# Chunked delta rule: token transpositions ahead of the first inverse level, and new values as the inverse times (values less decayed keys times state)

## What is computed

```python
    qc, kc, vc = to_chunks(q), to_chunks(k), to_chunks(v)
    decay = jnp.cumsum(gc, axis=-1)
    gamma = jnp.exp(jnp.where(incl, diff, -jnp.inf))
    kb = kc * bc[..., None]
    vb = vc * bc[..., None]
    a_mat = jnp.where(strict, jnp.einsum('bnhid,bnhjd->bnhij', kb, kc) * gamma, 0.0)
    t_mat = triangular_solve(eye + a_mat, eye, left_side=True, lower=True)
    u = jnp.einsum('bnhij,bnhjd->bnhid', t_mat, vb)
    w = jnp.einsum('bnhij,bnhjd->bnhid', t_mat, kb * jnp.exp(decay)[..., None])
    ...
    def step(S, inp):
        qd, kd, u_, w_, qk_, l_ = inp
        v_new = u_ - jnp.einsum('bhcd,bhde->bhce', w_, S)
        o = jnp.einsum('bhcd,bhde->bhce', qd, S) + jnp.einsum('bhij,bhje->bhie', qk_, v_new)
        S = S * l_[..., None, None] + jnp.einsum('bhcd,bhce->bhde', kd, v_new)
        return S, o
```

## Time and profile before

| | us |
|---|---|
| median of 3 runs | 1842.6 (1842.48 to 1845.2) |
| the profiled execution | 1842.54 |
| its span in the trace | 1840.8 |
| PE busy in the span | 1752.9 (95%) |
| DVE busy in the span | 834.1 (45%) |

### The profile page before, as it was taken

The page is one execution under the profiler, slowest core; times in us unless marked ns, Lnnn a source line. Parts: engine busy times, 40 slices in busy tenths (PEclk is TensorE's granted clock), DMA queues, the critical chain, the costliest instruction groups (busy, mean ns, idle before and its releaser), DMA issues.

```text
span 1840.8 us, 26847 instructions
## 1 busy us (share of the span) xinstructions
PE 1752.9 (95%) x10357; PEld 1404.9 (76%) x10357; DVE 834.1 (45%) x1436; ACT 675.7 (37%) x1414; POOL 710.8 (39%) x436
## 2 busy tenths in 40 slices
PE   6999999999997788999999999999999999999999
PEld 5888878877776674567877777888888888888887
DVE  4289878611126787565563354321331332233133
ACT  5366587688841223665045723010001001001000
POOL 4332234433344441563362235434334433442441
PEclk9999999999997999899999999999999999999999
DMA  7230111232212012002201001111111111111112
GB/s 237 59 80 24 35 35 46 58 99 74 91 47 82 2 60 103 1 2 92 69 28 53 24 23 46 46 46 48 54 34 57 46 49 53 46 46 46 57 34 91
DMA packets 112027, 102.33 MB, mean 56 GB/s; under 512 B 5131, under 2 KB 99390, under 8 KB 111678
## 3 DMA queue, kind: packets, MB, share of 16 engines
q1 hardware_dynamic: 109630, 92.67, 16.6%
q10 hardware_dynamic: 2304, 8.39, 1.1%
HBM read 87.42 MB, written 13.63 MB: 55 GB/s over the span
## 4 chain that ended last, share of the span: by engine, by line
PE 88%; DVE 6%; ACT 2%; issue 2%; POOL 1%; DMA 1%; DVEq 0%; ACTq 0%; POOLq 0%
PE ps L1445 9%; PE ps L1447 9%; PE ps L1446 9%; PE ps L437 7%; PE ps L439 7%; PE ps L438 7%; PE ps L409 6%; PE ps L410 6%; PE ps L411 6%; PE ps L987 2%; PE ps L1118 2%; PE ps L1276 2%; PE ps L1301 2%; PE ps L1287 2%; PE ps L939 2%
## 5 line engine op out<-in xcount | busy, mean ns | idle before, releaser
L754 POOL TENSOR_TENSOR WS<-WR,zero 128x1024 fp32r<-128x1024 f32 (+1 forms) x119 | 227.3, 1910 | 878.9 <-PE ps L411 299.0
L756 POOL TENSOR_TENSOR WS<-WR,WS 128x1024 fp32r<-128x1024 f32 (+1 forms) x119 | 302.3, 2541 | 9.3
L1445 PE MATMUL ps<-HS,WS 128*128 128x512 f32 x704 | 274.7, 390 | 3.2 <-DVE HS L345 3.2
L1447 PE MATMUL ps<-HS,WS 128*128 128x512 f32 x704 | 274.3, 390 | 0.0
L1446 PE MATMUL ps<-HS,WS 128*128 128x512 f32 x704 | 274.2, 389 | 0.0
L456 DVE TENSOR_TENSOR X<-X,ps 128x512 f32<-128x512 f32 x272 | 184.6, 687 | 155.9 <-PE ps L439 155.9
L409 PE MATMUL ps<-HS,WS 128*128 128x512 f32 (+2 forms) x560 | 215.4, 385 | 3.9 <-ACT raw L1569 3.9
L410 PE MATMUL ps<-HS,WS 128*128 128x512 f32 (+2 forms) x560 | 212.6, 380 | 0.0
L411 PE MATMUL ps<-HS,WS 128*128 128x512 f32 (+2 forms) x560 | 212.2, 379 | 0.0
L2278 DVE TENSOR_TENSOR prod<-sil,ps 128x512 f32<-128x512 f32 x44 | 30.2, 687 | 394.7 <-PE ps L1447 394.7
L1796 ACT ACTIVATE sil<-ps 128x512 f32<-128x512 f32 x44 | 26.3, 598 | 395.0 <-PE ps L1447 395.0
(11 more groups left out here) (308 smaller groups left out, 2991.6 us busy)
## 6 DMA issues: line engine op xcount, KB each, us to landing
WR<-in_w_gu SPq DMA_DIRECT2D x44, 512.0 KB, 3.8
WR<-in_w_in SPq DMA_DIRECT2D x36, 512.0 KB, 3.7
WR<-in_w_down SPq DMA_DIRECT2D x22, 512.0 KB, 3.6
X<-in_x SPq DMA_DIRECT2D x8, 1024.0 KB, 8.3
dsa_spill<-cacc ACTq DMA_DIRECT2D x12, 512.0 KB, 2.6
KW<-in_w_xkv SPq DMA_DIRECT2D x8, 512.0 KB, 5.0
WR<-in_w_out SPq DMA_DIRECT2D x8, 512.0 KB, 3.7
out<-X SPq DMA_DIRECT2D x8, 512.0 KB, 2.6
```

The lines of the kernel that those rows point to most:

```text
L754: pool.tensor_tensor(hi, w, bc(zero1[:, 0:1], [P, cols]), ALU.add).then_inc(w_hi, 1)
L756: pool.tensor_tensor(lo, w, hi.bitcast(F32), ALU.subtract).then_inc(w_split, 1)
L1445: pe.matmul(ps[:, b0 + half, :], lo, HS[:, 0, k, c], start=(k == 0), stop=False)
L1447: mm = pe.matmul(ps[:, b0 + half, :], hi, HS[:, 0, k, c], start=False, stop=(k == KT - 1))
```

## The change

The parts of batches 1 to 3 come in another order: `k` and `v` now stand before the levels, in `PREP`; batch 0 keeps its order in `FIRST`. Part `w`, `nkbd` and `wTt` are gone. In their place a new step `of_keys` multiplies the keys by the state on PE into a free part of a PSUM bank (four matmuls a chunk), and DVE forms `rhs` from it (two instructions of 128x128: times `ned`, plus `vb`); `new_v` is then a single product of the inverse with `rhs`. In the scan of a chunk `of_keys` and `from_state` come first, then a part, `new_v`, a part, `to_state`, a part, `out`, a part. Because `kD` is loaded over the keys early, ACT copies the keys of chunks 8 to 15 into `kept` once (part `rest` of batch 0). POOL masks level 1 (`X1`) before it makes `Xm`, the first `Am` waits for one slice less (`hs_done` 3 instead of 4), `threshold`'s counts move from parts 10 to 14 of batch 0 to parts 13 to 15, and some entries of `MASKS` move by one part. ACT's `squares` run after `from_state` instead of `new_v`. SP's three loads wait for the same parts, the last for `TT5` in place of `w1`.

```diff
-        PREP = (["gq", "x0"] + [f"{x}{s}" for s in (1, 2, 3) for x in "yz"]
-                + ["k", "y4", "z4", "v", "y5", "z5", "w", "next"])
+        FIRST = (["gq", "x0"] + [f"{x}{s}" for s in (1, 2, 3) for x in "yz"]
+                 + ["k", "y4", "z4", "v", "y5", "z5", "rest", "next"])
+        PREP = ["gq", "k", "x0", "v"] + [f"{x}{s}" for s in LV for x in "yz"] + ["rest", "next"]
+        def tok_bank(b, part, j):
+            return (0 if b and part == "k" else 3) if j else 1
...
             for c in range(SEQ // CHUNK):
-                run(new_v, c)
+                run(of_keys, c)
+                run(from_state, c)
                 if c < 12:
                     b, parts = c // 4 + 1, PREP[4 * (c % 4):4 * (c % 4) + 4]
                     prep(b, parts[0])
+                    run(new_v, c)
+                    prep(b, parts[1])
                     run(to_state, c)
-                    prep(b, parts[1])
-                    run(from_state, c)
                     prep(b, parts[2])
                     run(out, c)
                     prep(b, parts[3])
                 else:
                     tail(2 * (c - 12))
+                    run(new_v, c)
                     run(to_state, c)
-                    run(from_state, c)
                     run(out, c)
                     tail(2 * (c - 12) + 1)
...
             gp.wait(sp, "k1", 3)
+            sp.wait_ge(keys_kept, 1)
             sp.dma_start(kD[:, :, :], back[1]).then_inc(qk_in[1], 16)
...
-            gp.wait(sp, "w1", 3)
+            gd.wait(sp, "TT5", 3)
             sp.dma_start(qD[:, :, :], back[0]).then_inc(qk_in[0], 16)
...
                     gd.wait(pool, "A", b)
+                    level(b, 1)
                     if b == 0:
                         pool.wait_ge(hs_done, 4)
...
-                elif part == "w":
-                    gd.wait(pe, "TT5", b)
-                    for ul in range(8):
-                        for par in range(2):
...
-                            mm = pe.matmul(ps[:, 2 + par, c], nkbd[r, ul * P:(ul + 1) * P], TTm[r, B, c],
...
+            def of_keys(c):
+                if c == 0:
+                    return
+                if c == 8:
+                    pe.wait_ge(keys_kept, 1)
+                sd_.wait(pe, "S", c - 1)
+                for ul, hl, hh, r in pairs_of(c):
+                    w0, h = c % 8 * P + CHUNK * hh, 2 * hh + hl
+                    k = both(4, hl)[:, w0:w0 + CHUNK] if c < 8 else kept[:, hl, w0:w0 + CHUNK]
+                    mm = pe.matmul(ps[r, 6, (2 + hl) * P:(3 + hl) * P], k, S[:, c % 2, h * P:(h + 1) * P],
+                                   start=(hl == 0), stop=(hl == 1), skip_group_check=True)
+                kp_.mark(mm, "ks", c - 1)
...
+                else:
+                    qa_.wait(pe, "qs", c - 1)
+                    rd_.wait(pe, "rhs", c - 1)
+                for ul, hl, hh, r in pairs_of(c):
+                    v = rhs[r, hl * P:(hl + 1) * P] if c else vb[r, B, ul * P:(ul + 1) * P]
+                    mm = pe.matmul(ps[r, 4, hl * P:(hl + 1) * P], TTm[r, B, ul * CHUNK:(ul + 1) * CHUNK], v,
+                                   start=(hl == 0), stop=(hl == 1), skip_group_check=True)
...
+                elif part == "rest" and b == 0:
+                    for hl in range(2):
+                        ins = act.activation(kept[:, hl, :], both(4, hl)[:, SEQ:2 * SEQ], ACT.Copy)
+                    ins.then_inc(keys_kept, 1)
...
-            MASKS = {15: [(2, "count"), (2, "tie")], 16: [(2, 0), (2, 1)], 17: [(2, "kept"), (2, "out")],
+            MASKS = {15: [(2, "count"), (2, "tie")], 16: [(2, 0), (2, 1)], 17: [(2, "kept")], 18: [(2, "out"), (2, "bias")],
...
-                if p == 10:
+                if p == 13:
...
+                    for hl in range(2):
+                        ul = 2 * (c % 4) + hl
+                        ins = dve.scalar_tensor_tensor(rhs[:, hl * P:(hl + 1) * P], ps[:, 6, (2 + hl) * P:(3 + hl) * P],
+                                                       ned[:, 2 * c + hl:2 * c + hl + 1],
+                                                       vb[:, c // 4 % 2, ul * P:(ul + 1) * P], ALU.mult, ALU.add)
```

More of the change, by code:

```diff
@@ L92, in sem, with steps @@
             return ctx.enter_context(nc.semaphore(name))
-        def steps(name, names):
-            return Steps(sem(name), names)
+        def steps(name, names, first=None):
+            return Steps(sem(name), names, first)
         ps = ctx.enter_context(nc.psum_tensor("ps", [P, 8, BANK], F32))
@@ L179, in build_layer @@
         blk = at("blk", [P, 2, 8 * BANK], 56)
-        kdec, vb, wTt = (blk[:, :, 2 * i * BANK:2 * (i + 1) * BANK] for i in range(3))
+        kdec, vb = (blk[:, :, 2 * i * BANK:2 * (i + 1) * BANK] for i in range(2))
         TTm, QKm = blk[:, :, 6 * BANK:7 * BANK], blk[:, :, 7 * BANK:8 * BANK]
-        nkbd = at("nkbd", [P, 8 * P], 96)
+        kept = at("kept", [P, 2, SEQ], 88)
+        rhs = at("rhs", [P, 2 * P], 80)
         Tm = at("Tm", [P, BANK], 100)
@@ L594, in bc_bank, with gdn_order @@
             return e % 3 if e < 8 else e % 2
-        def gdn_order(prep, tail, new_v=None, from_state=None, to_state=None, out=None, beside=None):
+        def gdn_order(prep, tail, new_v=None, from_state=None, to_state=None, out=None, beside=None, of_keys=None):
             def run(step, c):
@@ L603, in gdn_order @@
             prep(-1, "next")
-            for part in PREP:
+            for part in FIRST:
                 run(beside, part)
@@ L1101, in prep @@
                     for j in range(2):
[L1102 to L1108, removed]
+                        bank, src = tok_bank(b, part, j), 4 if part == "k" else 8
+                        if b == 0:
+                            gd.wait(pe, f"kd{j}" if part == "v" else "Q", b)
+                        elif part == "k":
+                            if j:
+                                ga.wait(pe, "gam", b)
+                            else:
+                                gd.wait(pe, "TT5", b - 1)
+                        else:
+                            gd.wait(pe, "Q" if j else "kd0", b)
                         for q in range(4):
@@ L1261, in tail @@
                     o_tr(3 * (h - 5) // 2 + 2)
-            gdn_order(prep, tail, new_v, from_state, to_state, out, beside)
+            gdn_order(prep, tail, new_v, from_state, to_state, out, beside, of_keys)
             for t in range(T_ON, TT):
@@ L1638, in prep @@
                     ga.mark(act.activation(Ym[:, :], ps[:, 0, :], ACT.Copy), part, b)
-                elif part == "w":
-                    if b >= 2:
-                        sp_.wait(act, "o", 4 * (b - 1) - 1)
-                    for j in range(2):
-                        gp.wait(act, f"w{j}", b)
-                        ga.mark(act.activation(wTt[:, B, j * BANK:(j + 1) * BANK], ps[:, 2 + j, :], ACT.Copy),
-                                f"w{j}", b)
+                elif part == "rest" and b == 0:
+                    for hl in range(2):
+                        ins = act.activation(kept[:, hl, :], both(4, hl)[:, SEQ:2 * SEQ], ACT.Copy)
+                    ins.then_inc(keys_kept, 1)
             def squares(t):
@@ L2153, in prep_and_masks @@
                     dve.sem_inc(masks_made, 1)
-            gdn_order(prep_and_masks, tail, to_state=to_state, out=out)
+            gdn_order(prep_and_masks, tail, to_state=to_state, out=out, of_keys=of_keys)
             mean_o(1, T_ON, TT)
```

82 lines of the change are left out of this document (37 added, 45 removed).

## The result

| | kernel before | changed kernel |
|---|---|---|
| median, us | 1842.6 (4 runs, 1842.5 to 1845.2) | 1861.2 (4 runs, 1860.9 to 1862.4) |
| profiled execution, span, us | 1840.8 | 1859.1 |
| mean granted clock (1.00 is PE's full speed) | 0.976 | 0.963 |

The ratio is 1.0099, with a 95% interval of 1.0081 to 1.0116. The forecast was 9.3 us faster; it is 18.6 us slower (1.0%), outside the range and of the other sign.

What follows compares the result with a forecast made beforehand. PE, busy 95% of the span, was taken as the bound, so gains come from its work or waits. Terms summed to 11.3 us, less 2 for the clock: 9.3 gained, 1833.2 us, range 1827.5 to 1840.

Steps and rivals of the forecast that it cites:

- 1 first level: First level of batch 0: `Am` no longer waits for slice 3 and `y1` starts earlier; 2.7 us gained.
- 2 `z4` to `Am` 1: From `z4` of batch 0 to `Am` of batch 1: 18.98 us before, 14.1 after; 4.9 us gained.
- 3 batch 1: Batch 1, `Am` to `Am`: longer way to `z1`, shorter levels; 43.7 us before, 40.3 after, 3.4 gained.
- 4 batch 2: Batch 2: later `z1`, but no `w` product; 37.3 us before, 34.6 after, 2.7 gained.
- 5 batch 3 to chunk 12: Batch 3 to `to_state` of chunk 12: late `rhs` and square root; 37.4 us before, 38.9 after, 1.6 lost.
- 6 tail: Tail: `to_state` waits for ACT's `vn` in chunks 13 to 15, one `from_state` moved ahead; 0.8 us lost.
- reserve of 0 to 4 us for the clock: Batches 2 and 3: products slower after the new waits; 2 us taken off the gain, between 0 and 4.
- wrong sign: At chunk 12, a stall of more than 3 us would show the forecast wrong.
- The price of `rhs`: DVE's two `rhs` steps a chunk: between 0.5 and 1.7 us, taken as 0.55.
- The rule that speaks against it: Mask steps beside POOL's products ahead of `y1` run longer: two meetings a batch at 0.8 us, 4.8 us, giving 1838.0.
- The one that ended slower: One more passage per chunk, `rhs` late by 1.2 us in all 15 chunks: 18 us lost, 1849; chance 0.09.
- Rival c: POOL and DVE meet and PE is cold after each stall: 1838.0 us; chance 0.18.

Runs made afterwards that it cites:

- filled pause: Changed kernel with five added float32 matmuls on PE around `new_v` of chunk 12, three before and two behind, output unread; 1839.5 us, ratio 0.9993.
- late square root: Changed kernel with tile 7's last three mask steps moved into the tail and ACT's square root moved from tail piece 0 to 1; 1834.9 us.
- first level alone: Kernel before, with only POOL making `X1` before `Xm` and `Am` waiting for one slice fewer; 1843.4 us, ratio 1.0013.

## Why the prediction was wrong, step by step

Against the profiled executions (us gained; the last product of the projection stood 0.7 us earlier after than before, which no step claims):

| step | predicted | measured | from |
|---|---|---|---|
| 1 first level | +2.7 | +2.6 | `z4` at 557.83 against 561.17, less 0.7 |
| 2 `z4` to `Am` 1 | +4.9 | +4.8 | 14.18 against 18.98 |
| 3 batch 1 | +3.4 | -0.9 | 44.58 against 43.73 |
| 4 batch 2 | +2.7 | +1.2 | 36.13 against 37.28 |
| 5 batch 3 to chunk 12 | -1.6 | -3.3 | 40.68 against 37.38 |
| 6 tail | -0.8 | -24.1 | 61.0 against 36.9 |
| projection, and behind the logits | 0 | +1.4 | 0.7 each |

**The step that failed** is the sixth, the tail, with the reserve of 0 to 4 us for the clock that was to cover it. I priced the clock by its cost behind one wait inside a batch (about 1.5 us), and in the tail I counted the waits on `vn` (0.48 us each, as measured) but not the clock at which its products run. Step 5 even forecast the late `rhs` and the square root ahead of `vn`. What a fall of the clock there costs stood nowhere in the sum: 32 us of PE work become 55. The filled pause measures it, 21.7 us with every path left as it was; with the clock up the tail took 37.8 us, so the 0.8 of the step (36.9 to 37.7) was right for that clock. That a gain at the end of chunk 15 passes through whole did hold, to 0.7 us. The fair comparison with the forecast of 1833.2 us is the kernel with the filled pause, 1839.5 us: 6.3 us above it, and only just inside the range. That the late square root gave 1834.9, 1.7 from the forecast, is luck, since it also took 3.5 us off the way to chunk 12, by clearing two waits that step 5 had counted as lost.

I had also named the wrong sign for it: a stall at chunk 12 of more than 3 us. The waits were 0.78 and 1.23 us, with PE busy 0.66 us in 2.3, and the clock fell in the second of them; the third, 0.47 us, came behind the fall. Small waits one behind the other were enough, while the kernel before passed the same seam with PE busy 3.3 to 3.8 us in each 4.

**Steps 1 and 2** were right to 0.1 us: `y1` at 539.10 (forecast 539.8, less 0.7 for the projection), the projection's matmuls at 0.39 to 0.40 us behind it, `Am` of batch 1 at 572.01 (572.5). Even so, the run with the first level alone shows that 2.7 us won there need not arrive: the same edit delays `Tm` in the later batches by 2.1 us in all, which step 1 left out, and dips of the clock took some 2.6 us more.

**Step 3** was right up to `z1` (`y1` 9.8 us after `Am`, forecast 9.3; `z1` 15.3, forecast 15.1), and 4.1 us short from `z1` to `Am` of batch 2: 29.3 us, not 25.2. I had walked the levels at the full clock. `z1` itself and `y2` ran at 1.95 and 1.80 us instead of 1.15, and there were waits of 1.23 us on POOL's mask at `y3` and of 1.20 us on `rhs` at chunk 2, behind which `z3` ran at 1.98. **Steps 4 and 5** missed by 1.5 and 1.7 us, step 5 behind the wait of 4.61 us at chunk 9. The price of `rhs` (0.55 us a pair) was right: pairs took 0.56 to 0.61.

**The rule that speaks against it.** A mask step beside POOL's products was again slower. DVE, a step of 512 columns beside POOL and one of 640 with POOL idle:

```profile
593.64 1.42 DVE L1937 SCALAR_TENSOR_TENSOR score<-tieW,negdist 128x512 f32<-128x512 f32 x1
...
609.33 0.82 DVE L1937 SCALAR_TENSOR_TENSOR score<-tieW,negdist 128x640 f32<-128x640 f32 x1
```

POOL at the same time (`Sl`, then a level mask), and its next level mask, beside `rhs` and small steps of DVE:

```profile
593.03 1.48 POOL L865 TENSOR_TENSOR Sl<-S,lastb 128x512 f32<-128x512 f32 x1 [7.89 <-DVE S L2096]
594.47 1.71 POOL L826 TENSOR_TENSOR gam<-Am,Lev 128x512 f32<-128x512 f32 x1
597.49 1.27 POOL L826 TENSOR_TENSOR gam<-Am,Lev 128x512 f32<-128x512 f32 x1 [1.30 <-PE ps L1135]
```

Both are longer, DVE by some 0.7 us (1.42 less 512/640 of 0.82) and POOL's mask by 0.4. The Trainium skill ("SBUF — State Buffer", section "SBUF: two separate sides") describes the shared port as an exclusive lock; these rows agree. But the kernel before has such steps too, and no run isolates the meetings, so how much of steps 3 to 5 is theirs stays open.

**The rivals.** The one that ended slower had the wrong mechanism: `rhs` late in all 15 chunks. It was late by over 2 us in chunks 1, 5 and 9, and elsewhere by at most 1.25 us. Its 1849 was also too low. Rival c had the clock, but only within the batches, and its 1838.0 comes near the 1839.5 of the filled pause. The missing rival was that of the seam: a pause before the tail, 24 us, decided by about 2 us of idle time. Its rows were in the trace of before: L1207 at 1.07 us with the clock at 1.00, and inside the batches single waits after which products ran at 1.97.

## What to carry to other kernels

Before moving a wait, look at what PE does behind it. Here a fall of the clock inside a batch cost one or two microseconds, but ahead of the long tail of small products it cost the whole stretch at half speed. (The products of the batches are small too, and the clock came back in them; what about the tail's keeps it down was not isolated, only that eight dense ones raised it.) Price each seam by that, as a case of its own and not as a reserve, and keep the work of other engines off whatever releases PE there. A change that makes room in a dependency chain may pay only when the side work is placed anew, as here, so judge it after that.

## What the runs showed of the hardware that was not expected

- The granted clock stayed at 0.50 for 61.0 us while PE was busy 54.6 of them. The Trainium skill ("TensorE: Matmul & The Clock Gate", "Part 1: The HAM clock gate") puts the penalty of the ramp, which it tells of a kernel's start, at less than 1% of a typical kernel's span. A fall in the middle is another case: here one cost 24.1 us of 1840.8, 1.3%.
- Five matmuls of 128x256 around `new_v` kept the clock up (21.7 us less); eight of them in the slow tail brought it back within 5.0 us, and it held for some 15 us and fell again without a wait of over 0.5 us.
- The same kernel, with the same waits, came in two groups 18 us apart, by whether the clock came back after 13 us in the tail or not. The changed kernel's four runs (1860.9 to 1862.4 us) and the two with the pause put into the kernel before (1868.6 and 1869.0) show no second group.
